# A two-block transformer kernel: queues written in another order, and the second block's output projection on unnormed outputs

## The reference, cut to what matters

```python
def first_block(...):
    for i in range(DEPTH):                                   # DEPTH = 2
        hx = rmsnorm(x, g_pre_mix[i]) * (1.0 + sc1) + sh1    # the context likewise: hc
        px = hx @ w_in[i]
        ...                                                  # attention, Fourier mixing, long convolution
        mix_x = jnp.concatenate([attn_x, four_x, hy_x], axis=-1) @ w_out[i]
        x = x + ga1 * rmsnorm(mix_x, g_post_mix[i])
        fx = rmsnorm(x, g_pre_ffn[i]) * (1.0 + sc2) + sh2
        yx = conv_ffn(fx, w_up[i], w_ffn_conv[i], b_ffn_conv[i], w_down[i])
        x = x + ga2 * rmsnorm(yx, g_post_ffn[i])

def second_block(...):
    proj = rms_norm(h, norm_mix_g) @ w_in
    y_dil = dilated_mixture_attention(...)                   # heads 0 to 7
    y_na = neighbourhood_attention(...)                      # heads 8 to 15
    y_dil = rms_norm(y_dil, g_out_dil)                       # over its 512 columns
    y_na = rms_norm(y_na, g_out_na)                          # over its 512 columns
    h = h + jnp.concatenate([y_dil, y_na], axis=-1) @ w_out
    h = h + hierarchical_moe(rms_norm(h, norm_ffn_g), ...)   # 16 experts, top 2 of one group
    return rms_norm(h, norm_final_g)
```

## Time and profile before

| what | value |
|---|---|
| median of 3 executions | 2690.38 us (2687.37 to 2690.76) |
| the profiled execution, whole | 2689.45 us |
| its span in the trace | 2687.6 us |
| PE busy | 2401.5 us, 89% |
| DVE, ACT, POOL busy | 49%, 40%, 24% |
| mean granted clock of TensorE | 0.931 of full |
| DMA | 291 MB, 108 GB/s on the mean, 340 in the last eighth |

### The profile page before, as it was taken

One profiled execution on the slowest core, in us unless ns is written; L12 is line 12 of the kernel. 1 busy time (PEld: TensorE's weight loads), 2 busy tenths in 40 slices (PEclk: granted clock), 3 DMA queues, 4 the chain that ended last, 5 costly groups with the idle time before them and its releaser, 6 DMA issues.

```text
span 2687.6 us, 31931 instructions
## 1 busy us (share of the span) xinstructions
PE 2401.5 (89%) x12232; PEld 1876.5 (70%) x12232; DVE 1320.9 (49%) x2071; ACT 1080.3 (40%) x1647; POOL 638.4 (24%) x285
## 2 busy tenths in 40 slices
PE   4997977979999999979887889999999998859998
PEld 3875834857888888867564567888867765547776
DVE  3436943134441344225386216525433288529998
ACT  4324621243332233225264035434332256427776
POOL 1220000132222222232200043444444400112223
PEclk8999968979999999979997889999999989979999
DMA  6430041103322232213302232323313311229997
...
DMA packets 81039, 291.29 MB, mean 108 GB/s; under 512 B 10713, under 2 KB 13050, under 8 KB 79932
## 3 DMA queue, kind: packets, MB, share of 16 engines
...
## 4 chain that ended last, share of the span: by engine, by line
PE 71%; DVE 14%; ACT 5%; DMA 3%; POOL 2%; DVEq 2%; issue 2%; ACTq 1%; SPq 0%; POOLq 0%
PE ps L576 36%; PE ps L623 11%; DVE mlo L2287 4%; PE ps L1173 2%; PE ps L680 2%; PE ps L599 2%; DVE stat L1875 2%; DVE ptl L1891 2%; PE ps L1063 2%; POOL x L538 1%; PE ps L1191 1%; DVE pr L1883 1%; PE ps L1014 1%; PE ps L920 1%; DMA wraw<-in_w_all 1%
## 5 line engine op out<-in xcount | busy, mean ns | idle before, releaser
L532 POOL TENSOR_TENSOR wlo<-wraw,whi 128x1024 fp32r<-128x1024 f32 x208 | 502.5, 2418 | 1789.3 <-ACT whi L1213 1129.9
L576 PE MATMUL ps<-hhi,whi 128*128 128x512 f32 x1624 | 593.1, 365 | 9.6 <-POOL wlo L532 7.6
L576 PE MATMUL ps<-hlo,whi 128*128 128x512 f32 x1624 | 586.6, 361 | 0.0
L576 PE MATMUL ps<-hhi,wlo 128*128 128x512 f32 x1624 | 583.4, 359 | 0.0
L576 PEld LDWEIGHTS ps<-hhi,whi 128*128 128x128 f32 x1624 | 308.5, 190 | 80.6 <-issue 27.3
L576 PEld LDWEIGHTS ps<-hhi,wlo 128*128 128x128 f32 x1624 | 307.3, 189 | 48.1
L576 PEld LDWEIGHTS ps<-hlo,whi 128*128 128x128 f32 x1624 | 308.3, 190 | 46.1 <-issue 1.0
L1756 DVE SCALAR_TENSOR_TENSOR up<-ps,cconv,up 128x511 f32<-128x511 f32 (+1 forms) x132 | 83.2, 658 | 282.5 <-ACT up L1504 280.1
L2287 DVE TENSOR_TENSOR mlo<-mraw,mhi 128x1024 fp32r<-128x1024 f32 x147 | 205.7, 1429 | 7.1 <-ACT mhi L1636 7.0
L1220 ACT ACTIVATE whi<-wraw 128x1024 fp32r<-128x1024 f32 x132 | 139.0, 1053 | 127.5 <-PE ps L623 125.9
L623 PE MATMUL ps<-alo,whi 128*128 128x512 f32 (+1 forms) x528 | 188.0, 356 | 0.0
...
## 6 DMA issues: line engine op xcount, KB each, us to landing
...
```

The costliest lines, as they stand in the source:

```text
L532: pool.tensor_tensor(wlo[:, slot, :], wraw[:, AT_W[n] % RING, :], whi[:, slot, :].bitcast(F32), ALU.subtract).then_inc(lo_split, 1)
L576: m = pe.matmul(ps[:, bank + b, 0:w], a, r[:, c0:c0 + w], start=k == 0 and q == 0, stop=k == KT - 1 and q == 2)
```

## The change

1. **Output projection of the second block.** In the attention loop ACT now writes each output tile twice: out_hi, gain applied and rounded, and its square without gain; DVE's output_low makes the low part one step later. POOL adds the squares of each half's four tiles; output_sums on PE makes them columns, at step 50 for the first half and after four row parts for the second. Behind the loop PE goes on with row parts of unnormed outputs. After k = 3 DVE takes the first half out of PSUM, times its 1/rms, plus x; k = 4 starts PSUM anew, and the second half is taken out likewise.
2. **spread.** DVE writes rdiag, the identity scaled by rcol, in two halves; PE multiplies ones by it.
3. **norm_apply.** ACT writes nfull for the first 512 tokens only; in norms of 768, DVE writes the other 256 itself, with a drain behind.
4. **y** is cleared by POOL behind the postmix additions, not by DVE behind the preffn norm.
5. **Table loads.** load_sqrt before the last output tile and before the last down tile; a dummy Silu at each chunk's start, a dummy Exp before the first block's attention.
6. **Splits.** The last one of the output projection behind the square roots; at a chunk's first two tiles before the evacuation, and the wait for cconv behind the first; at the second block's start, the first two between the norm's steps.
7. **First block's attention.** vth, and DVE's values_lo, behind the first step's exponentials and minima; the five DMA issues (now the function filter_tables) in step 4.
8. **Second block's start.** below and namask are issued at tile 4, tables at tiles 6 and 8.

```diff
+def out_hi(k):
+    return px2r[:, 12 * (k // 4) + 4 + k % 4, :]
+def out_lo(k):
+    return px2r[:, 12 * (k // 4) + 8 + k % 4, :]
+def out_sq(a, j):
+    return px2[:, 12 * a + j, :]
...
+            if key[1] == "postmix":
+                pool.drain()
+                pool.memset(y[:, :, 0:W], 0.0).then_inc(sem("y_clear"), 1)
...
+        if n == B2_SLAB + IN2_T + RING - 1:
+            for a in range(2):
+                for j in range(1, 4):
+                    pool.wait_ge(sem("osq_ready"), 4 * a + j + 1)
+                    m = pool.tensor_tensor(out_sq(a, 0), out_sq(a, 0), out_sq(a, j), ALU.add)
+                    if j < 3:
+                        pool.drain()
+                m.then_inc(sem("osum_ready"), 1)
...
-        pe.wait_ge(sem("rinv_ready"), nth(key) + 1)
-        for tt in range(width // P):
-            m = pe.matmul(psf[:, 3072 + tt * P:3072 + tt * P + P], rcol[:, tt:tt + 1].to_broadcast([P, P]), ident[:, :],
-                          start=True, stop=True)
+        rd = rdiag[:, :, :].rearrange("p t n -> p (t n)")
+        half = width // 2
+        for z in range(2):
+            pe.wait_ge(sem("rdiag_ready"), 2 * nth(key) + z + 1)
+            for c0, w, b in segs[width]:
+                a, e = max(c0, z * half), min(c0 + w, z * half + half)
+                if a < e:
+                    m = pe.matmul(ps[:, 6 + b, a - c0:e - c0], ones[:, :], rd[:, a:e], start=True, stop=True)
         m.then_inc(sem("r_ready"), 1)
...
+    def output_sums(a):
+        pe.wait_ge(sem("osum_ready"), a + 1)
+        for tt in range(4):
+            m = pe.matmul(ps[:, 5, 4 * a + tt:4 * a + tt + 1], out_sq(a, 0)[:, tt * P:tt * P + P], ones[:, 0:1],
+                          start=True, stop=True)
+        m.then_inc(sem("osum_used"), 1)
...
+        if i == 50:
+            output_sums(0)
...
-    for a in range(2):
-        pe.wait_ge(sem("attn_out"), 3 * NQT + 8)
-        for k in range(4):
-            pe.wait_ge(sem("osq_ready"), 4 * a + k + 1)
-            pe.matmul(ps[:, 4 + a, :], ones[:, :], nsq2[:, k % 2, :], start=k == 0, stop=k == 3)\
-              .then_inc(sem("osq_used"), 1)
...
-        hi, lo = hhi[:, k, tt * P:tt * P + P], hlo[:, k, tt * P:tt * P + P]
+        hi, lo = out_hi(k)[:, tt * P:tt * P + P], out_lo(k)[:, tt * P:tt * P + P]
...
-                m = pe.matmul(ps[:, 2 * tt + c, :], h, w(a, c), start=k == 0 and z == 0,
-                              stop=k == KT - 1 and z == 2)
+                m = pe.matmul(ps[:, 2 * tt + c, :], h, w(a, c), start=k % 4 == 0 and z == 0,
+                              stop=k % 4 == 3 and z == 2)
...
-    for k in range(ROW_K):
-        slab_ready(O0 + k)
-        pe.wait_ge(sem("out_h_ready"), k + 1)
-        for tt in range(TX // P):
-            m = row_part(tt, k)
-        m.then_inc(slab_done, 1)
-    pe.wait_ge(sem("out_h_ready"), KT)
+    slab_ready(O0)
+    for tt in (0, 1):
+        row_part(tt, 0)
+    slab_ready(O0 + 1)
+    for tt in (0, 1):
+        row_part(tt, 1)
+    output_sums(1)
+    pe.wait_ge(sem("attn_out"), 3 * NQT + 8)
+    row_part(3, 0)
+    pe.wait_ge(sem("ostd_ready"), 1)
+    row_part(2, 0).then_inc(slab_done, 1)
+    row_part(3, 1)
+    row_part(2, 1).then_inc(slab_done, 1)
+    slab_ready(O0 + 2)
+    for tt in range(4):
+        m = row_part(tt, 2)
+    m.then_inc(slab_done, 1)
+    slab_ready(O0 + 3)
+    for tt in range(4):
+        row_part(tt, 3).then_inc(sem("row_done") if tt < 3 else slab_done, 1)
+    slab_ready(O0 + 4)
+    for tt in range(4):
+        pe.wait_ge(sem("xrow_ready"), tt + 1)
+        m = row_part(tt, 4)
+    m.then_inc(slab_done, 1)
...
+    def load_sqrt():
+        act.activation(consts[:, 15:16], zero_c, ACT.Sqrt)
     def summed_rms(key, width):
...
+        split(B2_SLAB + RING)
         act.wait_ge(sem("sq_used"), (KT + 1) * sq_nth(key) + KT + 1)
         rms(key, width)
+        split(B2_SLAB + RING + 1)
...
-            for c0, w, b in segs[width]:
-                act.activation(nfull[:, k % 2, c0:c0 + w], nt[:, k % 2, c0:c0 + w], ACT.Identity,
-                               bias=bfn(k, b), scale=afn(k, b))
+            act.activation(nfull[:, k % 2, 0:TX], nt[:, k % 2, 0:TX], ACT.Identity, bias=bfn(k, 0), scale=afn(k, 0))
...
+        def filter_tables():
+            act.wait_ge(sem("k_roped"), 5 * L + 5)
...
+        def values_hi():
+            act.wait_ge(sem("vt_done"), L + 1)
...
+        act.activation(consts[:, 15:16], zero_c, ACT.Exp)
...
+            if i == 0:
+                values_hi()
+            if i == 4:
+                filter_tables()
...
+            if s == OUT_T - 1:
+                load_sqrt()
...
-            split(S0 + IN_T + s + RING)
+            if s < OUT_T - 1:
+                split(S0 + IN_T + s + RING)
...
         summed_rms((L, "postmix"), W)
+        split(S0 + IN_T + OUT_T - 1 + RING)
...
-            act.wait_ge(sem("cconv_ready"), i + (L * CHUNKS + 1))
             act.wait_ge(sem("ysq_ready"), i * KT + KT * ffn_nth(L))
+            act.activation(consts[:, 15:16], zero_c, ACT.Silu)
             for p in range(PAIRS):
                 for z in range(2):
                     s = 2 * p + z
                     b = bank2(G0 + s)
                     act.wait_ge(slab_done, i * FFN_SLABS + (F0 + s + 1))
+                    if p == 0:
+                        split_in(i, FFN_STEP[L], F0 + s + RING)
+                    if s == 0:
+                        act.wait_ge(sem("cconv_ready"), i + (L * CHUNKS + 1))
                     act.activation(up[:, p % 2, z, 0:W], psf[:, b * 512:b * 512 + W], ACT.Identity,
                                    bias=cconv[:, s, 3:4], scale=cconv[:, s, 1:2]).then_inc(sem("up_mid"), 1)
-                    split_in(i, FFN_STEP[L], F0 + s + RING)
+                    if p:
...
             for o in range(KT):
+                if o == KT - 1:
+                    load_sqrt()
...
-        split(n + RING)
+        if s >= 2:
+            split(n + RING)
+        if s == 4:
+            act.dma_start(below[:, :], dram["below"]).then_inc(sem("tables_in"), 16)
+            act.dma_start(namask[:, :], dram["namask"]).then_inc(sem("tables_in"), 16)
+        if s in (6, 8):
+            load_table(s // 2 - 3)
...
-            act.activation(px2[:, 12 * (tl // 4) + tl % 4, :], ps[:, 6 + tl % 2, :], ACT.Copy)\
-               .then_inc(sem("attn_out"), 1)
+            act.activation(out_hi(tl), ps[:, 6 + tl % 2, :], ACT.Copy, scale=vec[:, V2_OUT + tl:V2_OUT + tl + 1])\
+               .then_inc(sem("ohi_ready"), 1)
+            act.activation(out_sq(tl // 4, tl % 4), ps[:, 6 + tl % 2, :], ACT.Square).then_inc(sem("osq_ready"), 1)
...
-    act.wait_ge(sem("attn_out"), 3 * NQT + 8)
-    for a in range(2):
-        for k in range(4):
...
-        act.activation(nrm2[:, a, :], ps[:, 4 + a, :], ACT.Sqrt, bias=eps_c, scale=1.0 / 512)\
-           .then_inc(sem("ostd_ready"), 1)
-    for k in range(KT):
-        a = k // 4
-        act.wait_ge(sem("ot_ready"), k + 1)
-        src = px2[:, 12 * a + k % 4, :]
-        act.activation(hhi[:, k, 0:TX], src, ACT.Copy).then_inc(sem("ohi_ready"), 1)
+    act.wait_ge(sem("osum_used"), 2)
+    act.activation(ss[:, 0, 0:8], ps[:, 5, 0:8], ACT.Sqrt, bias=eps_c, scale=1.0 / 512).then_inc(sem("ostd_ready"), 1)
...
-        dve.reciprocal(rcol[:, 0:n], rcol[:, 0:n]).then_inc(sem("rinv_ready"), 1)
+        dve.reciprocal(rcol[:, 0:n], rcol[:, 0:n])
+        dve.drain()
+        for z in range(2):
+            t0, h = z * n // 2, n // 2
+            dve.tensor_tensor(rdiag[:, t0:t0 + h, :], ident[:, :].unsqueeze(1).to_broadcast([P, h, P]),
+                              rcol[:, t0:t0 + h].unsqueeze(2).to_broadcast([P, h, P]), ALU.mult)\
+               .then_inc(sem("rdiag_ready"), 1)
         dve.wait_ge(sem("r_ready"), nth(key) + 1)
...
+                if width == T:
+                    dve.wait_ge(sem("scaled_ready"), KT * pre_nth(key) + k)
+                    dve.tensor_scalar(nfull[:, (k - 1) % 2, TX:T], nt[:, (k - 1) % 2, TX:T], afn(k - 1, 1), bfn(k - 1, 1),
+                                      ALU.mult, ALU.add)
+                    dve.drain()
...
+            if i == 0:
+                values_lo()
...
-        dve.memset(y[:, :, 0:W], 0.0)
...
+            dve.wait_ge(sem("y_clear"), L + 1)
...
+    def output_low(tl):
+        dve.wait_ge(sem("ohi_ready"), tl + 1)
+        dve.wait_ge(sem("osq_ready"), tl + 1)
+        dve.scalar_tensor_tensor(out_lo(tl), ps[:, 6 + tl % 2, :], vec[:, V2_OUT + tl:V2_OUT + tl + 1],
+                                 out_hi(tl).bitcast(F32), ALU.mult, ALU.subtract).then_inc(sem("attn_out"), 1)
...
+        if i >= 14 and (i - 14) % 8 == 0:
+            output_low((i - 14) // 8)
...
-    for a in range(2):
-        dve.wait_ge(sem("ostd_ready"), a + 1)
-        dve.reciprocal(nrm2[:, a, :], nrm2[:, a, :])
-        dve.drain()
-        for k in range(4 * a, 4 * a + 4):
-            src = px2[:, 12 * a + k % 4, :]
```

(24 more changed lines are left out.)

69 lines of the change are left out of this document (30 added, 39 removed).

## The result

| | before | changed |
|---|---|---|
| median of 4 executions | 2689.94 us | 2670.41 us (2665.55 to 2675.64) |
| ratio | | 0.9925, 95% interval 0.9903 to 0.9948 |
| profiled execution, whole and span | 2689.45, 2687.6 us | 2675.64, 2673.8 us |
| PE busy; mean granted clock | 2401.5 us; 0.931 | 2409.8 us; 0.926 |

The change gains 19.5 us where 29.2 were forecast; the range held it. The profiled execution of the changed kernel is the longest of its four, 13.8 us under the one of before. These four lie 10 us apart, those of before 3.4: that spread is the first thing to explain.

What follows compares the result with a forecast made beforehand. PE's matmuls were taken to set most of the time (busy 2401.5 of 2687.6 us), leaving its stops and the low clock behind them to gain. The eight terms sum to -29.2 us, from 2690.4 to 2661.2; range 2646 to 2676.

Steps and rivals of the forecast that it cites:

- Output stage: Behind the second attention: row parts start where the last step's matmuls end; -19.8 us, bounds -21 and -15.
- start of the second block: Split ahead of rcol, PE resumes at 2017.4 instead of 2022.94, low clock gone; -8.6 us, bounds -5 and -9.
- chunk start: First FFN chunk: POOL clears y, split first, the 5.24 us stop goes; -7.8 us, bounds -3 and -10.
- roots: Postmix: a split and table load leave layer 1's path, a load layer 0's; -3.0 us, bounds -4 and -1.
- Attention loop: Second block: added ACT and DVE passes hide in the first half, four tiles pay 1.4 each; +6.5 us, bounds +1, +21.
- signs that I had named for being wrong: First-half windows over 19 us, PE waits over 2, norm-feed period over 2.4, loop clock under 0.95, longer experts' stage.
- the full price of the attention: Rival: added passes lengthen first-half steps too and POOL may block DVE; +20 instead of +6.5, 2675 us, chance 0.2.
- the rival for the slower side: Small PE stops in every step drop the clock to 1.2 GHz; half the loop gives 2727 us, chance 0.03.
- POOL's additions: Second attention loop: six additions of 1.43 us each, blocking DVE for that long in the +21 us bound.
- Spread: Seven norms on the path: a DVE product and drain ahead, +0.4 us each; +2.8 us, bounds -0.2 and +0.7 each.
- Norm feed: Three norms: DVE becomes the bound in place of ACT, 0.1 x 8 left; -2.7 us, bounds -8 and +1.
- First attention: First block: start gains 1.4 us in layer 0, step 4's DMA issues cost 2.9 and 1.9; +3.4 us, bounds 0, +6.

Runs made afterwards that it cites:

- tab_alone: Changed kernel with one edit: DVE makes the next head's tab in the last step of a head, not the third; 2658.26 us, ratio 0.9887.
- steps_apart: Changed kernel with ACT's rounded copy two steps later, its square four, DVE's low part five; 2653.70 us, ratio 0.9881.
- steps_apart_tab: As steps_apart, with DVE's low part one step earlier and tab made in a head's last step; 2652.44 us, ratio 0.9868.
- change_again: The changed kernel once more, no edit, against the kernel before; 2672.9 us, ratio 0.9941.
- only_part1: Kernel before with the new output stage (part 1) alone; 2693.60 us, ratio 1.002.
- filters_first: As old_spread, with filter_tables() called ahead of the dummy Exp, not in step 4; 2643.07 us, ratio 0.9823.
- old_spread: As steps_apart_tab, with the spread as before the change: matmuls of the broadcast column, no rdiag; 2644.26 us, ratio 0.9834.

## Why the prediction was right and wrong

Direction and range were right, and the forecast of 2661.2 was 9 us too low. The measured terms below add up to -13.0 us, beside -13.8 for the two profiled executions; they come from several kernels, so the sum is a check and no more.

- **Output stage, start of the second block, chunk start, roots**: -19.8, -8.6, -7.8, -3.0 forecast; -20.1, -8.4, -8.3 (7.1 in layer 0 and 1.2 in layer 1) and about -3 measured. Each was a stop of one engine with a named engine behind it, taken from one timeline, with what is late next worked out. The clock behind a stop came back as counted. At the chunk the credit went to the wrong edit: I argued from the cleared y, and the order of the split alone does it.
- **Attention loop**: the step that failed, +6.5 against +25.4. I set the added passes against the slack of eight steps taken together ("DVE has 2.6 us over and a pass takes 0.75 of it"), but the slack is one of each step, and the pass went into the step that was already the longest. It made a stop 1.05 us longer in the first half too, and 5.7 us in all where no low clock follows (tab_alone). steps_apart and steps_apart_tab show that most of the slack was there, for passes in other steps. And I wrote that "every new stop I can name is under 1.5 us", having looked at the old stops and the added work apart: the 1.21 us at tab steps and the 1.05 for a tile fall into the same step every second time, which makes 2.25, and behind these stops the clock goes down. The order of the queues had it; I didn't add the two. Of the signs that I had named for being wrong, two came: a window of 19.15 us in the first half, and a clock of 0.85 over the loop.
- **The rivals**: the full price of the attention (+20, 2675) gave nearly the right sum for the wrong reason, with the passes at 1.45 each; a tile's stop grew by 1.05. The rest was the mechanism of the rival for the slower side, in small: the clock, not over half the loop, but behind the four stops for 17 us in change_again's profile and 34 in the first one. For the output stage alone it did end on the slower side (only_part1).
- **POOL's additions** took 1.29 us each, not 1.43, and blocked DVE once in the profiled execution. DVE and POOL of the changed kernel:

```profile
2303.37 1.58 DVE L2178 TENSOR_SCALAR p<-p,stat 128x512 f32<-128x512 f32 x1
```

```profile
2303.37 1.29 POOL L557 TENSOR_TENSOR px<-px 128x512 f32<-128x512 f32 x1 [22.63 <-ACT px L1651]
```

A product that takes 0.49 us took 1.58 when both started at once, and PE waited 0.36 for it. The Trainium skill ("SBUF — State Buffer", section "Who interferes with whom") has it so: DVE's fast modes and GpSimd exclude each other. The trace agrees, at one of the six additions, and its price was 0.4 us and not the 8.6 of the bound.
- **Spread**: +2.8 forecast, about +8 measured, beyond the bound of +0.7 for each norm. DVE's product and drain cost 0.64, within the bound of 0.7; the low clock that they bring, and the stop behind the loop's jump, were on no row.
- **Norm feed**: -2.7 forecast, -5.9 measured, inside the bounds. DVE's 256 columns took 0.41, and the period fell by 0.18 us for each k, not 0.1, in three norms, with less low clock behind.
- **First attention**: +3.4 forecast, about -0.7 measured: of the issues in step 4 only 1.07 us reached DVE.

The best version run is filters_first or old_spread, which can't be told apart: the change with the old spread, the three output operations in three different steps and tab in a head's last step; 2643.1 and 2644.3 us, 1.7% faster than the kernel before and 26 to 27 us faster than the change.
